# Query projections and five gate tiles computed between the units of two attentions

## What is computed

```python
aq, ak, av, bq, bk, bv, cq, cf, cb, ci, cg, gates = features(h_lat, w_in[l], qn_b[l], kn_b[l], rope)
yc = hgrn2_bidir(cq, cf, cb, ci, cg, ...)             # scan branch, times silu(cg)
ya = window_attn(aq, ak, av, cak, cav, sink_a[l])     # local attention "A", with a sink
yb = global_attn(bq, bk, bv, cbk, cbv)                # global attention "B", all 768 keys
x_mix = x + m_lat[:, :, 2] * merge_branches(ya, yb, yc, gates, w_branch[l], w_out[l])

def merge_branches(ya, yb, yc, gates, w_branch, w_out):
    up = einsum('blnw,nwd->blnd', stack([ya, yb, yc], 2), w_branch)
    g = sigmoid(gates.reshape(B_, L, 3, -1))
    return sum(g * up, axis=2) @ w_out
```

## Time and profile before

| | |
|---|---|
| median of 3 runs | 3074.35 us |
| the profiled execution | 3073.83 us |
| its span | 3072.0 us |
| TensorE busy | 94% of the span |
| VectorE busy | 50% |
| ScalarE busy | 39% |
| GpSimd busy | 11% |
| mean granted TensorE clock | 0.978 of full speed |

### The profile page before, as it was taken

One profiled execution on the slowest core, in us unless ns is written; L12 is line 12 of the kernel. 1 busy time (PEld: TensorE's weight loads), 2 busy tenths in 40 slices (PEclk: granted clock), 3 DMA queues, 4 the chain that ended last, 5 costly groups with the idle time before them and its releaser, 6 DMA issues. The chain is left out here.

```text
span 3072.0 us, 38676 instructions
## 1 busy us (share of the span) xinstructions
PE 2877.8 (94%) x14576; PEld 2276.1 (74%) x14576; DVE 1550.9 (50%) x2177; ACT 1205.9 (39%) x1797; POOL 332.9 (11%) x286
## 2 busy tenths in 40 slices
PE   6999887999989999899999989999899999899998
PEld 2889665688868888686687768888576777678886
DVE  3467246555535443447753454443468663544434
ACT  3642424532233332334643343333425652333333
POOL 0020004500001110001200121100102102111100
PEclk8999999999999999999999999999999999999999
DMA  6100210045412222121032112222120131122222
GB/s 241 69 28 1 89 55 1 1 159 172 163 69 96 96 96 96 67 80 42 29 111 96 55 69 96 96 105 96 57 81 15 56 138 41 69 84 97 99 103 92
DMA packets 43552, 254.04 MB, mean 83 GB/s; under 512 B 4608, under 2 KB 6784, under 8 KB 15872
## 3 DMA queue, kind: packets, MB, share of 16 engines
q1 hardware_dynamic: 43392, 251.87, 22.9%
HBM read 249.75 MB, written 2.10 MB: 82 GB/s over the span
## 5 line engine op out<-in xcount | busy, mean ns | idle before, releaser
L250 DVE TENSOR_TENSOR ring_lo<-ring,ring_hi 128x2048 fp32r<-128x2048 f32 x201 | 460.7, 2292 | 795.5 <-ACT ring_hi L243 795.2
L243 ACT ACTIVATE ring_hi<-ring 128x2048 fp32r<-128x2048 f32 x201 | 383.8, 1909 | 459.0 <-PE bank L301 341.6
L301 PE MATMUL bank<-h_hi,ring_hi 128*128 128x512 f32 x1360 | 541.6, 398 | 19.4 <-DVE ring_lo L250 8.5
L301 PE MATMUL bank<-h_hi,ring_lo 128*128 128x512 f32 x1360 | 532.2, 391 | 0.0
L1535 PE MATMUL bank<-h_hi,ring_hi 128*128 128x512 f32 x960 | 374.1, 390 | 5.7 <-DVE ring_lo L250 5.7
L1539 PE MATMUL bank<-h_hi,ring_lo 128*128 128x512 f32 x960 | 373.5, 389 | 0.0
L1538 PE MATMUL bank<-h_lo,ring_hi 128*128 128x512 f32 x960 | 373.5, 389 | 0.0
L301 PEld LDWEIGHTS bank<-h_hi,ring_hi 128*128 128x128 f32 x1360 | 257.2, 189 | 79.2 <-issue 16.7
L301 PEld LDWEIGHTS bank<-h_hi,ring_lo 128*128 128x128 f32 x1360 | 256.9, 189 | 54.3
L301 PE MATMUL bank<-h_lo,ring_hi 128*128 128x512 f32 x624 | 243.9, 391 | 0.0
L1535 PEld LDWEIGHTS bank<-h_hi,ring_hi 128*128 128x128 f32 x960 | 180.2, 188 | 45.5 <-issue 5.5
(11 more groups left out here) (442 smaller groups left out, 4899.3 us busy)
## 6 DMA issues: line engine op xcount, KB each, us to landing
ring<-in_stream SPq DMA_DIRECT2D x209, 1024.0 KB, 4.8
mod_w<-in_stream SPq DMA_DIRECT2D x64, 256.0 KB, 4.5
xT<-in_xT SPq DMA_DIRECT2D x2, 2048.0 KB, 14.9
const<-in_const SPq DMA_DIRECT2D x1, 2306.5 KB, 16.3
par<-in_par SPq DMA_DIRECT2D x3, 696.0 KB, 3.9
memT<-in_memT SPq DMA_DIRECT2D x2, 1024.0 KB, 4.8
out<-xT SPq DMA_DIRECT2D x1, 2048.0 KB, 6.2
ctxT<-in_ctxT SPq DMA_DIRECT2D x1, 1024.0 KB, 4.8
```

The lines of the kernel that those rows point to most:

```text
L243: nc.scalar.activation(self.slab_hi(slab + j), self.slab(slab + j), ACT.Copy).then_inc(slab_rounded, 1)
L250: nc.vector.tensor_tensor(lower, self.slab(slab + j), self.slab_hi(slab + j).bitcast(F32), ALU.subtract)\
L301: ins = nc.tensor.matmul(out, lhsT, rhs, start=start and w is w_hi and x is x_hi, stop=stop and w is w_lo)
```

## The change

- The four query tiles of A leave the front stage, with their rotations and ropes. The tiles of `cg` move up to 14 to 17, the key logarithms from ScalarE's place 15 to 14, and the scan's gating goes to GpSimd.
- B runs before A. A new class `Beside` puts weight blocks between the attention's operations on TensorE, all into bank 7, one tile after the other. In B: the four query tiles of A and the first gate tile (40 blocks), with the rotations in units 1, 5, 9, 13 and three slabs rounded and halved. In A: four gate tiles (32 blocks), two slabs. `upto[u]` is how many blocks are done by unit u: 7 at once, then one to three a unit.
- The attention itself has three groups of transposes (tiles 0 to 3, 4 to 7, 8 to 11) but two banks for them: the third group shares bank 4 with the first and waits for its copy. The weight blocks stand between the second and the third group. VectorE copies groups 0 and 2, ScalarE group 1. Masks and sink are added for both heads (and both sides) at once. Values go to bank 6.
- The merge begins with one gate tile and six branch tiles, for which slabs are put together from pieces (`MERGE_PIECES`, up to four DMAs a slab), then goes on in pairs as before. ScalarE makes the five sigmoids of the early gates before its first read-out (`first_sigmoids`). Operands are split in the order B, scan, A. `load_mod` and the modulation steps are spread over 43 tiles instead of 48.

The diff, cut to its core:

```diff
-        def paired_attention(name, pairs, unit_of, read_out, work, slots, turn_banks, out_banks, copier, sink=None):
+        class Beside:
+            def products(self, pe, u):
+                while self.blocks < self.upto[u]:
+                    m, k = divmod(self.blocks, KT)
+                    if k == 0 and m > 0:
+                        if m <= len(self.turns):
+                            pe.wait_ge(self.by_sin.sem, self.by_sin.at(m))
+                        else:
+                            pe.wait_ge(self.tile_read.sem, self.tile_read.at(m))
+                    last = ws.mm(pe, self.tiles[m]["at"] + k, 1, bank[:, 7, :], (h_hi[:, k, :], h_lo[:, k, :]), True, k == 0, k == KT - 1)
+                    if k == KT - 1:
+                        last.then_inc(self.tile_done.sem, 1)
+                    self.blocks += 1
+            def scalar(self, act, u):
+                while self.read < self.upto[u] // KT:
+                    tile = self.tiles[self.read]
+                    act.wait_ge(self.tile_done.sem, self.tile_done.at(self.read + 1))
+                    nc.scalar.activation(tile["out"], bank[:, 7, :], ACT.Copy, scale=tile["scale"]).then_inc(self.tile_read.sem, 1)
+                    self.read += 1
+                if u in self.rounds:
+                    ws.round_to(act, self.rounds[u], ws.limit)
+            def sines(self, dve, u):
+                if u in self.turns:
+                    ...
+                    nc.vector.tensor_tensor(self.spare, bank[:, 7, :], self.table[:, 1, :], ALU.mult).then_inc(self.by_sin.sem, 1)
+            def vector(self, dve, u):
+                if u - 1 in self.turns:
+                    out = self.tiles[self.turns.index(u - 1)]["out"]
+                    nc.vector.tensor_tensor(out, out, self.table[:, 0, :], ALU.mult)
+                    dve.drain()
+                    nc.vector.tensor_tensor(out, out, self.spare, ALU.add)
+                if u in self.rounds:
+                    ws.halve_to(dve, self.rounds[u], ws.limit)
...
+                scores(0)
+                beside.products(pe, 0)
+                for u in range(N):
+                    if u + 1 < N:
+                        scores(u + 1)
+                    if u > 0:
+                        values(u - 1)
+                    beside.turn(pe, u)
+                    transposes(u, 0)
+                    transposes(u, 1)
+                    beside.products(pe, u + 1)
+                    transposes(u, 2)
+                values(N - 1)
...
+                for u in range(N):      # ScalarE
+                    if u + 1 < N:
+                        exps(u + 1)
+                    ...
+                    nc.scalar.activation(probsT[:, u % 2, first * P:end * P], bank[:, 5, 0:(end - first) * P], ACT.Copy)\
+                        .then_inc(probs_out[1].sem, 1)
+                    beside.scalar(act, u + 1)
...
+                for u in range(N):      # VectorE
+                    dve.wait_ge(exp_done.sem, exp_done.at(2 * (u + 1)))
+                    nc.vector.reciprocal(stat[:, u % 2, 2, :], stat[:, u % 2, 1, :]).then_inc(inverse_ready.sem, 1)
+                    if u + 1 < N:
+                        maxima(u + 1)
+                    if u % TB == 0 and u:
+                        turn_out(u // TB - 1)
+                    beside.sines(dve, u)
+                    copy(u, 0)
+                    copy(u, 2)
+                    beside.vector(dve, u + 1)
...
-                tiles += [("act", T, weights_still(F0 + (8 + n) * KT, KT, h), act_copy(qkA[:, n, :], scale=HD ** -0.5)) for n in range(4)]
-                        ("act", 7): lambda act: log_rows(act, QUERY[:2]), ("act", 9): key_squares, ("act", 15): key_logs,
+                        ("act", 7): lambda act: log_rows(act, QUERY[:2]), ("act", 9): key_squares, ("act", 14): key_logs,
+                linear("front", tiles, banks=6, sync=load_x, outs=outs, also=also, pe_also=pe_also, pool_also=gate_scan)
...
+            upto = [7, 8, 10, 12, 14, 16, 18, 20, 22, 24, 26, 28, 30, 32, 34, 37, 40]
+            beside = Beside(queries + first_gates[:1], upto, (1, 5, 9, 13), {1: FRONT + 7, 8: MERGE, 15: MERGE + 1}, axial, rope_spare[:, :])
+            attend("B", 1, False, qkB, kB, vab[:, :, P:2 * P], work, beside)
+            upto = [7, 9, 11, 13, 15, 17, 19, 21, 23, 25, 27, 28, 29, 30, 31, 32, 32]
+            beside = Beside(first_gates[1:], upto, (), {3: MERGE + 2, 11: MERGE + 3})
+            attend("A", 0, True, qkA, kA, vab[:, :, 0:P], work, beside)
...
+            def first_sigmoids(act):
+                for g in range(GATES_FIRST):
+                    nc.scalar.activation(gates[:, g, :], gates[:, g, :], ACT.Sigmoid).then_inc(gates_ready.sem, 1)
+            gate_tile(5, M0 + 40)
+            branch_tile(1, M0 + 48, True)
+            branch_tile(4, M0 + 52, True)
+            branch_tile(2, M0 + 56, False)
+            branch_tile(5, M0 + 60, False)
+            branch_tile(0, M0 + 64, False)
+            branch_tile(3, M0 + 68, False)
+            gate_tile(6, M0 + 72, len(tiles) - 2)
+            branch_tile(6, M0 + 80, True)
```

More of the change, by code:

```diff
@@ L40 @@
 LAYERS = 2
+GATES_FIRST = 5
 MEM = 256
@@ L1079, in paired_attention @@
+        def paired_attention(name, pairs, unit_of, read_out, work, beside, sink=None):
             units = [unit_of(t, tb) for t in range(pairs) for tb in range(TB)]
             N = len(units)
-            G = len(turn_banks)
+            OUT = 6
+            thirds = [0]
+            for unit in units:
+                thirds.append(thirds[-1] + (unit["keys"] > 4))
             scored = Signal("scored", N)
@@ L1110, in scores, with transposes @@
                             lhsT, rhs = operands[g]
-                            last = nc.tensor.matmul(head_scores(u, g)[:, lo:hi], lhsT, rhs, start=True, stop=True)
+                            last = nc.tensor.matmul(S[:, g, lo:hi], lhsT, rhs, start=True, stop=True)
                     last.then_inc(scored.sem, 1)
[L1114 to L1125, removed]
+                def transposes(u, b):
+                    if b >= len(groups(u)):
+                        return
+                    _, first, end = groups(u)[b]
+                    if b == 2:
+                        pe.wait_ge(probs_out[0].sem, probs_out[0].at(u + 1))
+                    elif u > 0:
+                        pe.wait_ge(probs_out[b].sem, probs_out[b].at(u))
+                        if b == 0 and thirds[u]:
+                            pe.wait_ge(probs_out[2].sem, probs_out[2].at(thirds[u]))
+                    for x in range(first, end):
+                        g, j = divmod(x, units[u]["keys"])
+                        if j == 0 or x == first:
+                            pe.wait_ge(probs_ready.sem, probs_ready.at(2 * u + g + 1))
+                        last = nc.tensor.transpose(bank[:, (4, 5, 4)[b], (x - first) * P:(x - first + 1) * P],
+                                                   probs[:, u % 2, g, j * P:(j + 1) * P], con("ident"))
+                    last.then_inc(turned[b].sem, 1)
@@ L2760, in add_branch, with gate_tile @@
                 return read_out
-            for n in range(KT):
-                for b in range(3):
-                    at = B1_AT["merge"] + (3 * n + b) * (KT + 4)
-                    tiles.append(("act", T, weights_still(at, KT, h), act_copy(gates[:, (3 * n + b) % 6, :], ACT.Sigmoid)))
-                    tiles.append(("dve", T, weights_still(at + KT, 4, ys[b]), add_branch(n, b), len(tiles) - 1))
+            def gate_tile(g, at, *before):
+                tiles.append(("act", T, weights_still(at, KT, h), act_copy(gates[:, g % 6, :], ACT.Sigmoid)) + before)
@@ L2766, in build_program @@
+            TILES = len(tiles)
             mod_w = tmp("mod_w", [P, MOD_BUFFERS, 512], here)
```

282 lines of the change are left out of this document (142 added, 140 removed).

## The result

The changed kernel takes 3081.18 us (median of 18 runs, 3078.39 to 3084.56), the kernel before 3074.38 (18 runs, 3071.80 to 3076.14): ratio 1.0022, 95% interval 1.0015 to 1.0029. So it is slower by 6.8 us, 4.2 more than forecast and just past the bound of 6 us that the prediction drew round "same"; the interval (0.15% to 0.29%) lies on both sides of that bound.

What follows compares the result with a forecast made beforehand. TensorE bounds the merge; in B a loop of scores, maxima and exponentials, in A VectorE's masks and maxima. Outside -56.2, attentions +54.7, gaps and clock +4: +2.5 on 3074.35, 3077 us; range 3055 to 3090.

Steps and rivals of the forecast that it cites:

- Front, -29.0: Front stage: four query tiles, their rotations and a TensorE stall leave, GpSimd's gating costs 0.7: 29.0 us shorter.
- the stall of 3.14: Front: TensorE's 3.14 us wait for key logarithms before the first rotation goes, as ScalarE takes them earlier.
- Merge, -27.2: Merge stage: five gate tiles leave a stretch that TensorE fills, 27.2 us shorter.
- the cover of 0.9: Merge start: weight slabs are rounded and halved before TensorE wants them, with 0.9 us to spare.
- rival 3: Merge goes late at its start, VectorE behind on mod steps and branch tiles: +4, 3081; chance 0.15 together with Rival 2.
- B, 123.5 with its barrier: Global attention B: late reciprocal makes TensorE wait for GpSimd; 81.7 us grows by 41.8, plain units 6.03.
- A, 94.4 to its last copy: Local attention A: plain units 4.85, three waits for the gates' PSUM bank, two units behind halvings; growth 13.0 us.
- Gaps and clock, +4: Additions to the queues' sum that the trace does not show: 2 us for matmul-kind changes, 2 for the clock.
- Clock, 2 taken: Both attentions: waits bring stretches at TensorE's lower clock, the fall at A's start goes; +2 us, bounds -2 to +12.
- Gaps, 2 taken: Both attentions: TensorE changes between weight blocks and transposes twice a unit; +2 us, bounds 0 to 5.
- Rival 1: Attentions: TensorE's work alone sets the pace, growth 19, result 3037, half of it 3058; chance 0.20, whole or half.
- Rival 2: Attentions: waits lower the clock for a sixth, switches at upper bound, about 3089; chance 0.15 together with rival 3.

Runs made afterwards that it cites:

- experiment 4: Kernel before with only ScalarE's key logarithms moved ahead of its copy of tile 14 in the front: 3070.63 us, ratio 0.9989.
- experiment 7: Changed kernel with ten more matmuls of 512 columns at the end of the front stage, ahead of B: 3084.09 us, ratio 1.0028.
- experiment 2: Changed kernel with A's weight blocks one earlier in each unit, so gate tiles end at a unit's end: 3080.39 us, ratio 1.0022.
- experiment 1: Changed kernel with VectorE's reciprocal of the next unit moved ahead of the last transposes' copy, ropes and halvings: 3063.97 us, ratio 0.9965.
- the fastest kernel: Changed kernel with reciprocal and A's blocks earlier, halvings in two, ten extra matmuls at the ends of front and merge: 3052.56 us, ratio 0.9931.
- experiments 2 and 3: experiment 2, and the changed kernel without the two rope operations on A's queries in B: 3081.24 us, ratio 1.0025.

## Why the prediction came out as it did

**Front, -29.0: right** (-29.2 from S). The four tiles, the rotations and the stall of 3.14 are all there, the last shown alone by experiment 4. GpSimd's last gating took 1.26 where VectorE's took 0.69, as priced from the earlier trace rows, and PE's wait for VectorE at the last rotation is 0.9 where I had 0.7.

**Merge, -27.2: right** (-27.3). PE waits there for nothing but its barrier, so the cover of 0.9 before the first slab held, and rival 3 did not come.

**B, 123.5 with its barrier, was 128.3.** The structure was right unit by unit; the terms, predicted and measured:

| unit of B | predicted | measured | times |
|---|---|---|---|
| first | 6.25 | 8.13 | 1 |
| second | 4.60 | 4.67 | 1 |
| u = 1, behind tile copy and halving | 10.5 | 11.79 | 1 |
| plain | 6.03 | 6.09 | 5 |
| with a rotation | 6.64 | 6.89 | 3 |
| behind a rope | 7.43 | 7.46 | 3 |
| behind a halving | 8.47 | 8.36 | 1 |
| last scores to the first of A | 21.4 | 21.8 | 1 |

Of the first unit's 1.9 the clock has 1.6, by experiment 7. u = 1 ran at 0.53 to 0.61 where it was late. The rotation's 0.25 is mine: beside early reciprocals it still costs 6.92 - 5.80 = 1.12 on PE, its 0.94 and the changes to and from it, and I let the wait for GpSimd hide more of it than it does.

**A, 94.4 to its last copy, was 99.9.** The masks, which the trace of before did not show in their new form, take 0.41 to 0.43 for 256 columns and 0.70 for 512 (0.34 and 0.61 taken, bounds 0.25 and 0.69), some 0.1 a unit where the loop of maxima and exponentials sets the pace. Three waits for the gates' bank are there: units of 7.19, 6.73 and 6.73, where I had 6.70. The two units behind a halving took 8.68 and 8.63, not 7.8: 1.7 too little. Both are the predicted mechanism with the lower clock on top: PE stands at the transposes for GpSimd (2.27 and 2.96), whose reciprocal stands behind the halving, and what follows runs at 0.50, from 585 in the first (the rows above) and from 632.8 in the second, whose halving starts 0.7 later after its scores:

```profile
632.80:636.20 3.40, 3.25 (x13) 2.14 (x12) 0.96 (x3) 1.74 (x5) 2.52 (x3) 0.50 0.02 5
```

The nine plain units are 45.9 together, not 43.7. The longest, 6.02, stood behind the first bank wait at the lower clock (4.94 in experiment 2, where that wait is gone). Two more, 5.30 and 5.29, are the same there and 4.94 with the early reciprocal: the late reciprocal reaches plain units of A too, which I had not seen. The first unit has 0.3 of the miss, and the 0.9 that I took off for the method's error should have stayed, as the new units did not come out shorter than laid out.

**Gaps and clock, +4: what came beyond the queues' sum was 10.5.** Here lie the 6.5 that the growth came out above the sum: 65.3 against 54.8 from the queues, where I had added 4. Taken apart by units, as an estimate:

- Clock, 2 taken: about 6 at most. The attentions have six stretches at the lower level, from 428.0, 448.5, 547.4, 567.9, 585.0 and 632.8; the units that they stand in exceed their terms by 1.6, 1.3, 0.4, 1.1, 0.9 and 0.8. By the granted shares the clock took 5.1 + 5.0 = 10.1 us of PE's time at most; before it was 6.6 + 1.6 = 8.2. So the clock fell hardly more than before, but now more of what ran slowly was on the path.
- Gaps, 2 taken: 0.3, the 0.06 by which five plain units exceed theirs. As long as the unit waits for GpSimd the changes between kinds of matmul hide in that wait.
- The rest, some 4, is neither: rotations, plain units of A, bank waits, and the 0.9 above. They are errors of the queue layout.

The clock's share lies in the range that I gave (-2 to +12). I took +2 because the fall at the start of the old A "should go". It did not go: with seven blocks behind it, the first unit still ran at half rate, because the wait that pulls the clock down is the barrier's, ahead of the blocks. The Trainium skill, "TensorE: Matmul & The Clock Gate", section "HAM oscillation — how this bites in real kernels", tells of a kernel whose TensorE waits for a transfer in every step and starts each next step at the lower clock, and its advice is to restructure the loop so that TensorE "stays warm". Experiment 7 gets there by added matmuls and agrees for the unit behind the barrier (8.13 to 6.51); it also shows a limit: in its profiled execution longer waits follow, and the fall comes at one of them.

**Not foreseen: the stage behind the merge.** It has the same work in all twelve traces, and took 47.6, 49.2 or 50.5 us. In before it was 49.2, with a stretch at half rate, in after 47.6 with none: 1.6 of luck on the side of the change, in these two profiled executions. This is the row of before:

```profile
826.00:829.00 3.00, 3.00 (x8) 2.33 (x8) 3.00 (x6) 3.00 (x5) 0.00 (x0) 0.50 0.73 273
```

**The rivals.** Rival 1 (PE alone, or half of it at 3058) did not come in the changed kernel, but it is what experiment 1 makes of B: 5.80 a unit, no wait for GpSimd. Its whole, 3037, was too low even so: in the fastest kernel the attentions still take 199.2 (110.8 + 88.4), 17 more than the 182 of that rival (162.9 + 19). Rival 2 (clock) had 17 beyond the queues where 10.5 came, and of these about 6 are the clock's by the estimate above: right in kind and too large. Both tests that were to show the mechanism through its parts (experiments 2 and 3) gave their unit its predicted length and the program almost nothing; only removing the cause common to 14 units did. That the total came near the forecast is in part luck: the misses of the attentions (+6.5) were eased by 2.2 in the stages behind them, of which the prediction had nothing.

## What to carry to other kernels

An operation of 0.15 us that another engine waits for belongs at the earliest place in its in-order queue where its input is there, ahead of every copy, rope or rounding that is put beside it: here its place alone decided between 7 us lost and 10 us won. A wait of 1 to 3 us in a stream that TensorE just fills can be paid again as lower clock (the changed kernel's attentions have six such stretches), and taking away one such wait may only move that payment: in experiments 2 and 3 alone nothing was left of it, beside the early reciprocal experiment 2's was worth 2.4. Compare stages from a mark ahead of the change, not spans, and look whether a gain stands in the stage that was edited. Small steps that can be had alone (the logarithms' place, -3.1 us) should be timed alone, because a large change hides them.

## What the runs showed of the hardware

The fall of the granted clock behind a barrier does not follow from the wait alone: behind the merge, ahead of the same matmuls and with PE idle 2.28 us and then 0.45 or 0.34, there was none in after, three us at 0.50 in before, six in experiment 2; the stage took 47.6, 49.2 and 50.5. What decides is not in these traces. Executions of one kernel differ in their clock too: in experiment 7 they lie nine us apart, with mean granted clocks of 0.979 and 0.976 to 0.977, and in experiment 1 the run of 3058.30 had 0.981 where the other four, near 3064, had 0.978 or 0.979. Ten matmuls of 512 columns in the first barrier removed the fall of B's first unit in all three kernels that had them. Behind the merge, where they cut the idle time to 0.69 us, there was no fall either, but there was none in three kernels without them. A program whose PE work was cut by 49 us ran the attentions at 0.86 and 0.80 of the full clock instead of 0.96 and 0.95. And a VectorE operation with two SBUF inputs that started inside a GpSimd instruction lasted to about 0.55 behind its end (a rope operation 1.36 instead of 0.68), a halving 3.00 instead of 2.29.
